# Router logits as fp32r products of split parts, and the last row tile's scaling split between two engines

## The chip, the cores and the metric

One Trainium2 chip, one NeuronCore, one launch. The metric is device time in microseconds (us) of that core, the median of a few runs; lower is better. Five engines work side by side: TensorE (PE; its weight loads have rows of their own, PEld), VectorE (DVE), ScalarE (ACT), GpSimd (POOL) and SyncE (SP, which only issues DMAs here). Each takes its instructions in order and they meet at semaphores.

## The reference, cut to what matters

One layer of a decoder on 1040 prompt rows (16 learned rows and 1024 prompt rows) and 8 sample rows, 1048 in all. After the mixer come the output projection, the residual sum, a norm, and a mixture of experts. Before the experts a router picks for each row one of 4 groups and two of its 8 experts:

```python
x = x + jnp.concatenate([y_a, y_b], axis=-1) @ w_out
h2 = rmsnorm(x, norm_ffn)
lg = h2 @ rg_w + rg_b                      # 4 group logits
le = h2 @ re_w + re_b                      # 32 expert logits
_, gsel = lax.top_k(lg, 1)
ev, ei = lax.top_k(le[group gsel], 2)
wts = softmax(lg)[gsel] * softmax(ev)
out = sum over the two experts e: wts * (silu(h2 @ w_gate[e]) * (h2 @ w_up[e])) @ w_down[e]
```

## The kernel before

The program runs in stages. The mixer fills the first 465 us. The stage that the change touches, `route_parts`, runs from 465 to about 612 us. The experts follow until about 970 us: 32 experts, whose weights stream in from DRAM while TensorE multiplies.

In `route_parts` the 1048 rows are cut into nine tiles, t = 0 to 8, eight of 128 rows and a last one of 24 (`LAST`). The order on each engine is written out by hand:

- TensorE, for tile t, runs eight steps i of six products with 512 columns each (line 2075: the output projection, as fp32r products of a high and a low part of each operand). Between the steps it does work on earlier tiles: at i = 2 `turn(t-1)` transposes the residual row tile (line 2002), at i = 3 `position(t-2)` counts rows per expert (2018, 2021), at i = 4 `score(t-1)` makes the logits (2010), at i = 6 `tabulate(t-2)` writes a table (2027). In tiles 1 and 2 it also carries products for the eight sample rows (1496, 1502).
- VectorE, for tile t, makes `yt_lo` of tile t+2 (1808, 1813), then the residual sum `x` (1913), then waits for the norm's factor and makes the normed rows `h` (1922), then `place(t-1)` (1887 to 1892), then `choose(t)` (1839 to 1881): some 25 small instructions, each waiting for the one before it, that turn logits into chosen experts. In tile 1 `sample.second` (1426 to 1429) stands between `h` and `place`.
- ScalarE makes the high parts for tile t+2 (1745, 1748), then the sum of squares (1774), its logarithm (1776) and exponential (1779), then copies the transposed tile from PSUM into `xtt` (1732, two copies of 512 columns), then two small exponentials for `choose`.

The score of a tile waits for both copies of `xtt`. The transpose of tile t waits for `x` of tile t. At the third tile `position(0)` also waits, through `sample.second_read`, until `sample.second` is done, since both use one PSUM bank. After the ninth tile's product (`prod` reaches 9) SyncE starts the first experts' weights, and what is left of the ninth tile (residual sum, transpose, score, choose, place, tabulate) has to end before the rows of the first experts can be gathered.

## Time and profile before

| | us |
|---|---|
| median of 3 runs | 981.25 (979.59 to 982.6) |
| the profiled execution, its own time | 979.38 |
| its span in the trace | 977.6 |
| TensorE busy in the span | 946.4 |
| VectorE busy | 698.6 |
| ScalarE busy | 491.2 |

The span runs from the first to the last instruction of the profiled execution; 1.8 us lie around it. Matmuls are pipelined, so a busy TensorE is not one at its peak, and a row's duration on TensorE holds a fill and drain that the next one overlaps: spacings of starts tell what one costs. The granted TensorE clock was 0.994 of full speed over the span.

### The profile page before, as it was taken

To read this page: it belongs to the slowest core of one execution; us is meant where nothing else is said; L and a number is where in the kernel's file an instruction comes from. 1 tells how busy PE (TensorE), PEld (TensorE's weight loads), DVE (VectorE), ACT (ScalarE), POOL (GpSimd) and SP (SyncE) were. 2 spreads that over 40 slices of the span, in tenths; PEclk is the share of its full clock that TensorE was granted. 3 is DMA by queue.
4 is the path that set the end of the run, shared out by engine and by line. 5 is a ranking of instruction groups with operands and counts; after the bars stand their busy time and mean duration, and the time that the engine had idled before them with its cause. 6 is when DMAs were issued, how large, how long until landed. Compare 5 with 4: busy or idle time off the path is not lost.

```text
span 977.6 us, 14810 instructions
## 1 busy us (share of the span) xinstructions
PE 946.4 (97%) x5408; PEld 817.8 (84%) x5408; DVE 698.6 (71%) x1059; ACT 491.2 (50%) x890; POOL 191.5 (20%) x153
## 2 busy tenths in 40 slices
PE   5999999999899999999999998999999999999996
PEld 4889999999899999999888885667777777777762
DVE  7466677789453634546666666769999999999996
ACT  7578778432423222232422313246666666666794
POOL 2000000000000000000030001315555555554414
PEclk9999999999999999999999999999999999999999
DMA  7104775623755664446833235999999999999994
GB/s 253 52 22 136 176 160 134 176 88 128 229 135 151 166 165 116 123 145 185 290 103 124 71 112 199 345 407 415 412 415 409 409 400 415 396 413 411 393 396 161
DMA packets 123499, 230.61 MB, mean 236 GB/s; under 512 B 71528, under 2 KB 84386, under 8 KB 114734
## 3 DMA queue, kind: packets, MB, share of 16 engines
q1 hardware_dynamic: 108102, 202.69, 60.0%
q0 software_dynamic: 15264, 26.92, 7.4%
q8 instruction: 37, 0.61, 0.3%
q14 instruction: 24, 0.20, 0.1%
q10 hardware_dynamic: 72, 0.20, 0.1%
HBM read 205.33 MB, written 53.11 MB: 264 GB/s over the span
## 4 chain that ended last, share of the span: by engine, by line
PE 86%; DVE 8%; ACT 3%; DMA 1%; issue 1%; SPq 0%; POOL 0%; POOLq 0%; ACTq 0%; DVEq 0%
PE psum L1157 26%; PE psum L2421 12%; PE psum L2075 10%; PE psum L2511 8%; PE psum L2425 5%; PE psum L2357 3%; PE psum L2405 3%; DVE xi L961 2%; DVE it L959 2%; PE psum L2478 2%; PE psum L1180 2%; PE psum L2010 1%; PE psum L1262 1%; DVE acc L901 1%; PE psum L1249 1%
## 5 line engine op out<-in xcount | busy, mean ns | idle before, releaser
L1157 PE MATMUL psum<-hh,wh 128*128 128x350 f32 x672 | 222.7, 331 | 0.7 <-ACT acc L690 0.7
L1157 PE MATMUL psum<-hh,wl 128*128 128x350 f32 x672 | 217.2, 323 | 0.0
L1157 PE MATMUL psum<-hl,wh 128*128 128x350 f32 x672 | 216.5, 322 | 0.0
L1157 PEld LDWEIGHTS psum<-hh,wh 128*128 128x128 f32 x672 | 127.1, 189 | 2.2 <-ACT acc L690 1.0
L1157 PEld LDWEIGHTS psum<-hl,wh 128*128 128x128 f32 x672 | 126.9, 189 | 0.9
L1157 PEld LDWEIGHTS psum<-hh,wl 128*128 128x128 f32 x672 | 126.6, 188 | 0.0
L2395 DVE TENSOR_TENSOR wgu_lo<-wgu,wgu_hi 128x1536 fp32r<-128x1536 f32 x60 | 105.4, 1758 | 17.1 <-ACT wgu_hi L2390 17.0
L2390 ACT ACTIVATE wgu_hi<-wgu 128x1536 fp32r<-128x1536 f32 x60 | 89.3, 1489 | 2.1 <-DMA new_ssm_sample<-s_in 2.1
L2421 PE MATMUL psum<-wgu_hi,xgt_hi 128*128 128x512 f32 x180 | 85.6, 475 | 0.0
L1702 POOL IOTA r_iw<- 128x8 f32 x1 | 0.1, 144 | 410.5 <-DMA mixer_rows<-th 410.5
L859 DVE TENSOR_TENSOR wl<-wst,wh 128x1024 fp32r<-128x1024 f32 x28 | 34.3, 1225 | 58.8 <-ACT wh L633 58.7
L2349 POOL DMA_INDIRECT sum_rows<-total,slot_rows x32 | 66.5, 2078 | 23.5 <-issue 22.1
L2421 PE MATMUL psum<-wgu_lo,xgt_hi 128*128 128x512 f32 x180 | 70.8, 393 | 0.0
L2421 PE MATMUL psum<-wgu_hi,xgt_lo 128*128 128x512 f32 x180 | 70.7, 393 | 0.0
L2491 DVE TENSOR_TENSOR wd_lo<-wd,wd_hi 128x2048 fp32r<-128x2048 f32 x30 | 68.8, 2292 | 1.2
L2118 POOL DMA_INDIRECT xg<-h_rows,slot_rows x34 | 63.5, 1869 | 24.3 <-DVE slot_rows L1933 10.3
L2343 POOL DMA_INDIRECT before<-sum_rows,slot_rows x34 | 34.4, 1012 | 149.2 <-DVE total L2524 142.9
L2487 ACT ACTIVATE wd_hi<-wd 128x2048 fp32r<-128x2048 f32 x30 | 57.7, 1923 | 0.0
L2425 PE MATMUL psum<-wgu,xgt_rest 128*128 128x512 f32 x120 | 56.3, 591 | 0.0
L2375 ACT ACTIVATE xgt_hi<-psum 128x768 fp32r<-128x768 f32 x30 | 24.4, 813 | 61.6 <-PE psum L2357 61.6
L901 DVE SCALAR_TENSOR_TENSOR acc<-raw,cqw,acc 128x1072 f32<-128x1072 f32 x36 | 48.0, 1334 | 0.9
L2075 PE MATMUL psum<-wo_hi,yt_hi 128*128 128x512 f32 (+1 forms) x144 | 47.8, 413 | 0.0
(376 smaller groups left out, 1887.5 us busy)
## 6 DMA issues: line engine op xcount, KB each, us to landing
wgu<-w_gate SPq DMA_DIRECT2D x34, 1024.0 KB
wgu<-w_up SPq DMA_DIRECT2D x34, 1024.0 KB
wd<-w_down SPq DMA_DIRECT2D x34, 1024.0 KB, 13.6
wst<-w_in SPq DMA_DIRECT2D x28, 512.0 KB, 4.2
ck<-qkv_rows SPq DMA_DIRECT2D x9, 702.0 KB
qkv_rows<-acc SPq DMA_DIRECT2D x12, 520.0 KB, 6.4
xb<-x SPq DMA_DIRECT2D x8, 512.0 KB, 4.3
wo<-w_out SPq DMA_DIRECT2D x8, 512.0 KB, 7.1
```

The source lines that it names most:

```text
L901: stt(ac[:, 0:QLEN], rw[:, q:q + QLEN], w[:, q:q + 1], ac[:, 0:QLEN], ALU.mult, ALU.add).then_inc(taps if q < KQ - 1 else conv_ok, 1)
L1157: ins = mm(ps[:, c, 0:ZC], w[:, kk, :], a[:, kk, c * ZC:(c + 1) * ZC], start=(kk == 0 and q == 0), stop=(kk == KD - 1 and q == 2))
L2075: ins = mm(ps[0:n, 2 * (t % 2) + c, :], y, w[:, c * 512:c * 512 + 512], start=(i == 0 and q == 0), stop=(i == KD - 1 and q == 2))
L2118: pool.indirect_dma_start(b.xg[k][:, :], None, b.h2_dram, bass.IndirectOffsetOnAxis(ap=b.slot_rows[:, e:e + 1].bitcast(U32), axis=0), boun ...
L2349: pool.indirect_dma_start(b.sum_d, rows_of(e), rows[:, :], None, bounds_check=TOK - 1, oob_is_err=False).then_inc(q.sum_out.sem, 16)
L2390: nc.scalar.activation(w_hi[x.p][h][:, :, :, :], half_of(b.slots[x.k][0], h), ACT.Copy).then_inc(w_hi_ok[h][x.p].sem, 1)
L2395: nc.vector.tensor_tensor(half_of(b.slots[x.k][1], h), half_of(b.slots[x.k][0], h), w_hi[x.p][h][:, :, :, :].bitcast(F32), ALU.subtract).t ...
L2421: ins = nc.tensor.matmul(gate_up_bank(x.p), a[:, kk, :], w, start=(kk == 0 and i == 0), stop=(kk == KP - 1 and i == 2))
L2425: nc.tensor.matmul(gate_up_bank(x.p), xt_rest[x.p][:, kk - KP, :], raw[:, :, kk, :], start=False, stop=False)
L2487: nc.scalar.activation(wd_hi[x.p][:, :, :], b.slots[x.k][2][:, :, :], ACT.Copy).then_inc(wd_hi_ok[x.p].sem, 1)
L2491: nc.vector.tensor_tensor(b.slots[x.k][3][:, :, :], b.slots[x.k][2][:, :, :], wd_hi[x.p][:, :, :].bitcast(F32), ALU.subtract).then_inc(wd_ ...
L2511: ins = nc.tensor.matmul(ps[0:C, 4 + 2 * x.p + c, :], h[x.p][:, f, :], w[:, f, c * 512:c * 512 + 512], start=(f == 0 and i == 0), stop=(f ...
```

## The change

The logits were f32 products of the transposed rows `xtt` (stationary, 128 x 128) and the weights `rwf` (36 columns). Now both are split into a part rounded to fp32r and the rest. The high parts of the rows multiply high and low weights side by side (72 columns), the low parts multiply the high weights (36 columns) and add to the first 36. VectorE makes the low part of the rows in `turned_low` and then joins the two halves of the logits with two instructions where it had one. Twice, at the start, VectorE works on the weights (`w_both`). In the ninth tile alone the normed rows are made otherwise: VectorE multiplies the rows by the weights of the norm, ScalarE scales the result by the norm's factor, and ScalarE copies the transposed rows before it takes the logarithm and the exponential.

```diff
-    xtt = m.place("xtt", [P, KD, P])
+    xtt = m.place("xtt", [P, KD, P], F32R)
+    xtt_lo = [m.place(f"xtt_lo{g}", [P, KD // 2, P], F32R, at=at) for g, at in enumerate((b.hist_at, b.state_at))]
+    w_both = m.place("r_w_both", [P, KD, 2, GRP + NE], F32R, at=b.negmask_at)
...
-            if t >= 2:
+            if 2 <= t < T - 1:
                 act.wait_ge(h2_out[t % 2], 16 * (t // 2))
-            a_(h2[t % 2][0:n, :], b.x1[0:n, t, :], ACT.Square, accum_out=b.stat[0:n, t, 0:1]).then_inc(sq.sem, 1)
+            scratch = h2[t % 2] if t < T - 1 else xt[1]
+            a_(scratch[0:n, :], b.x1[0:n, t, :], ACT.Square, accum_out=b.stat[0:n, t, 0:1]).then_inc(sq.sem, 1)
+            if t == T - 1:
+                copy_turned(t)
...
-            copy_turned(t)
+            if t < T - 1:
+                copy_turned(t)
             if t == T - 1:
+                act.wait_ge(rs.sem, rs.at(T))
+                act.wait_ge(weighted.sem, weighted.at(1))
+                a_(h2[0][0:n, :], h2[0][0:n, :], ACT.Copy, scale=b.stat[0:n, t, 2:3]).then_inc(h2_ok, 1)
                 act.wait_ge(h2_ok, T)
                 act.dma_start(b.h2_dram[8 * P:TOK, :], h2[0][0:LAST, :]).then_inc(h2_out[0], 16)
...
-            stt(lg[0:n, :], ps[0:n, 4, 0:GRP + NE], b.stat[0:n, t, 2:3], b.rb[0:n, :], ALU.mult, ALU.add
-                ).then_inc(lg_ok, 1)
-            dve.wait_ge(lg_ok, t + 1)
+            for q, base in enumerate((b.rb, lg)):
+                stt(lg[0:n, :], ps[0:n, 4, (GRP + NE) * q:(GRP + NE) * (q + 1)], b.stat[0:n, t, 2:3], base[0:n, :],
+                    ALU.mult, ALU.add).then_inc(lg_ok, 1)
+                dve.wait_ge(lg_ok, 2 * t + q + 1)
...
+        def turned_low(t):
+            n = rows(t)
+            if t == 0:
+                dve.wait_ge(b.hist_out, 16)
+                dve.wait_ge(b.state_out, 16)
+            for g in range(2):
+                dve.wait_ge(turned_c, 2 * t + g + 1)
+                tt(xtt_lo[g][:, :, 0:n], bank4(ps, 4 + g, P, n), xtt[:, 4 * g:4 * g + 4, 0:n].bitcast(F32), ALU.subtract
+                   ).then_inc(turned_lo.sem, 1)
...
         tt(rwf[:, :, :], b.rw[:, :, :], bc(wft[:, :], GRP + NE), ALU.mult).then_inc(rwf_ok, 1)
+        dve.wait_ge(rwf_ok, 1)
+        V.tensor_copy(w_both[:, :, 0, :], rwf[:, :, :]).then_inc(rwf_ok, 1)
+        dve.wait_ge(rwf_ok, 2)
+        tt(w_both[:, :, 1, :], rwf[:, :, :], w_both[:, :, 0, :].bitcast(F32), ALU.subtract).then_inc(rwf_ok, 1)
...
             if t == T - 1:
+                dve.wait_ge(x1_ok, T)
+                dve.wait_ge(h2_out[0], 16 * 4)
+                tt(h2[0][0:n, :], b.x1[0:n, t, :], wf[0:n, :], ALU.mult).then_inc(weighted.sem, 1)
+                turned_low(t)
                 place(t - 1)
+                dve.wait_ge(rs.sem, rs.at(T))
+                choose(t)
+                break
...
             stt(h2[t % 2][0:n, :], b.x1[0:n, t, :], b.stat[0:n, t, 2:3], wf[0:n, :], ALU.mult, ALU.mult
                 ).then_inc(h2_ok, 1)
+            turned_low(t)
             if t == 1:
                 sample.second(dve)
...
         def score(t):
             n = rows(t)
-            pe.wait_ge(turned_c, 2 * t + 2)
+            pe.wait_ge(turned_lo.sem, turned_lo.at(2 * t + 2))
             for kk in range(KD):
-                ins = mm(ps[0:n, 4, 0:GRP + NE], xtt[:, kk, 0:n], rwf[:, kk, :], start=(kk == 0), stop=(kk == KD - 1))
+                if kk >= 1:
+                    j = kk - 1
+                    mm(ps[0:n, 4, 0:GRP + NE], xtt_lo[j // 4][:, j % 4, 0:n], w_both[:, j, 0, :], start=False, stop=False)
+                if kk == KD - 1:
+                    mm(ps[0:n, 4, 0:GRP + NE], xtt_lo[1][:, 3, 0:n], w_both[:, kk, 0, :], start=False, stop=False)
+                ins = mm(ps[0:n, 4, 0:2 * (GRP + NE)], xtt[:, kk, 0:n], w_both[:, kk, :, :].rearrange("p k e -> p (k e)"),
+                         start=(kk == 0), stop=(kk == KD - 1))
             ins.then_inc(logits, 1)
```

The order of the instructions around it, at three places. First VectorE in the second tile (t = 1), before the change: `h` is the normed rows, the four rows of lines 1426 to 1429 are `sample.second`, 1887 and 1892 are `place(0)`, 1839 begins `choose(1)`. What stands in brackets is what the instruction waits for.

```order
L1922 SCALAR_TENSOR_TENSOR h_189<-x_158,stat,wf 128x1024 [waits x1_act]
L1426 TENSOR_TENSOR uu<-vu,psum 128x32 [waits s_products]
L1427 TENSOR_TENSOR oo<-uu,psum 128x32 [waits s_vec]
L1428 TENSOR_TENSOR oo<-oo,psum 128x32 [waits s_vec]
L1429 TENSOR_TENSOR osq_s<-oo 128x32 [waits s_vec]
L1887 TENSOR_TENSOR r_tmp_194<-r_o_200,psum 128x64 [waits r_pos,s_vec]
L1889 TENSOR_REDUCE r_rank<-r_tmp_194 128x2 [waits r_rank]
L1892 TENSOR_TENSOR r_in_slot<-r_rank,r_ic 128x256 [waits r_vec]
L1839 SCALAR_TENSOR_TENSOR lg<-psum,stat,rb 128x36 [waits logits]
L1847 TENSOR_REDUCE r_one<-lg 128x1 [waits lg_ok]
```

The same place on VectorE in the changed kernel (its line numbers are its own):

```order
L1956 SCALAR_TENSOR_TENSOR h_189<-x_158,stat,wf 128x1024 [waits x1_act]
L1904 TENSOR_TENSOR xtt_lo_191<-psum,xtt 128x512 [waits x1_copied]
L1904 TENSOR_TENSOR xtt_lo_192<-psum,xtt 128x512 [waits x1_copied]
L1427 TENSOR_TENSOR uu<-vu,psum 128x32 [waits s_products]
L1428 TENSOR_TENSOR oo<-uu,psum 128x32 [waits s_vec]
L1429 TENSOR_TENSOR oo<-oo,psum 128x32 [waits s_vec]
L1430 TENSOR_TENSOR osq_s<-oo 128x32 [waits s_vec]
L1910 TENSOR_TENSOR r_tmp_197<-r_o_203,psum 128x64 [waits r_pos,s_vec]
L1912 TENSOR_REDUCE r_rank<-r_tmp_197 128x2 [waits r_rank]
L1915 TENSOR_TENSOR r_in_slot<-r_rank,r_ic 128x256 [waits r_vec]
L1851 SCALAR_TENSOR_TENSOR lg<-psum,stat,rb 128x36 [waits logits]
L1851 SCALAR_TENSOR_TENSOR lg<-psum,stat,lg 128x36 [waits lg_ok]
```

Two subtractions that wait for ScalarE's copies now stand between `h` and `sample.second`, and a second instruction on the logits follows the first. The same two subtractions and the second logit instruction stand in every tile.

Second, VectorE in the ninth tile of the changed kernel:

```order
L1940 TENSOR_TENSOR x_158<-psum,xt_181 24x1024 [waits out_prod,x2_in0,r_vec]
L1947 TENSOR_TENSOR h_188<-x_158,wf 24x1024 [waits h2_out0,x1_ok]
L1904 TENSOR_TENSOR xtt_lo_191<-psum,xtt 128x4x24 [waits x1_copied]
L1904 TENSOR_TENSOR xtt_lo_192<-psum,xtt 128x4x24 [waits x1_copied]
L1910 TENSOR_TENSOR r_tmp_197<-r_o_203,psum 128x64 [waits r_pos]
L1912 TENSOR_REDUCE r_rank<-r_tmp_197 128x2 [waits r_rank]
L1915 TENSOR_TENSOR r_in_slot<-r_rank,r_ic 128x256 [waits r_tabled,r_vec]
L1851 SCALAR_TENSOR_TENSOR lg<-psum,stat,rb 24x36 [waits logits,x1_act]
L1851 SCALAR_TENSOR_TENSOR lg<-psum,stat,lg 24x36 [waits lg_ok]
```

Before, the three instructions of `place(7)` came straight behind `x`, and then `h`, which waited for the norm's factor; now the product with the weights alone comes first, and the factor is waited for by the logits.

Third, TensorE at the score of the second tile in the changed kernel. The semaphore `x_in0` counts the low halves that VectorE has made; before, these places held eight f32 products of 36 columns, the first waiting for `x1_copied`.

```order
L2050 MATMUL psum<-r_w_both,xtt 128x72 [waits x_in0]
L2047 MATMUL psum<-r_w_both,xtt_lo_191 128x36
L2050 MATMUL psum<-r_w_both,xtt 128x72
L2047 MATMUL psum<-r_w_both,xtt_lo_191 128x36
L2050 MATMUL psum<-r_w_both,xtt 128x72
```

## Rows read from the trace of the kernel before

**Rows 1.** The page: busy time of each engine over the span.

```profile
PE 946.4 (97%) x5408; PEld 817.8 (84%) x5408; DVE 698.6 (71%) x1059; ACT 491.2 (50%) x890; POOL 191.5 (20%) x153
```

**Rows 2.** Chain that ended last, 455 to 660 us: start, us, what.

```profile
544.49 0.87 PE psum L2002 x8
...
548.59 1.71 PE psum L2010 x16
...
559.09 0.87 PE psum L2002 x8
...
599.98 1.22 DVE x L1913
...
610.81 0.66 PE psum L2027 x4
```

**Rows 3.** Busy time in a stretch of the experts: PE, PEld, DVE, ACT, POOL, clock, DMA.

```profile
700.00:750.00 50.00, 50.00 (x225) 38.16 (x224) 46.09 (x43) 32.71 (x37) 27.44 (x17) 1.00 1.02 414
```

**Rows 4.** VectorE and the sixth tile's surroundings, 542 to 559 us, order of time.

```profile
545.62 1.28 DVE L1922 SCALAR_TENSOR_TENSOR h<-x,stat,wf 128x1024 f32<-128x1024 f32 x1 [1.78 <-ACT stat L1779]
...
548.20 1.98 PEld L2010 LDWEIGHTS psum<-rwf,xtt 128*128 128x128 f32 x16
...
550.34 0.26 DVE L1839 SCALAR_TENSOR_TENSOR lg<-psum,stat,rb 128x36 f32<-128x36 f32 x1 [2.24 <-PE psum L2010]
...
557.35 1.22 DVE L1913 TENSOR_TENSOR x<-psum,xt 128x1024 f32<-128x1024 f32 x1
...
558.70 1.02 PEld L2002 LDWEIGHTS psum<-ident,x 128*128 128x128 f32 x8
```

**Rows 5.** Weight loads by line (ns min/median/max), and the ninth tile's score.

```profile
L2010 PEld LDWEIGHTS psum<-rwf,xtt x144: 99/192/192, 485.1 to 603.7; 128*128 128x128 f32 x128, 128*24 128x24 f32 x16
...
L2075 PEld LDWEIGHTS psum<-wo_hi,yt_hi x144: 101/188/192, 464.9 to 598.3; 128*128 128x128 f32 x128, 128*24 128x24 f32 x16
...
603.25 0.70 PE L2010 MATMUL psum<-rwf,xtt 128*24 128x36 f32 x16 [0.24 <-ACT xtt L1732]
```

**Rows 6.** VectorE in the mixer's first stage: two subtractions of 512 columns from PSUM.

```profile
14.31 1.28 DVE L854 TENSOR_TENSOR hl<-psum,hh 128x512 fp32r<-128x512 f32 x2
15.51 1.22 DVE L859 TENSOR_TENSOR wl<-wst,wh 128x1024 fp32r<-128x1024 f32 x1
```

**Rows 7.** Timelines of DVE, ACT, PEld and PE around the third tile's start.

```profile
499.96 0.18 DVE L1426 TENSOR_TENSOR uu<-vu,psum 128x32 f32<-128x32 f32 x1
500.61 0.38 DVE L1429 TENSOR_TENSOR osq_s<-oo 128x32 f32<-128x32 f32 x1
506.27 0.25 DVE L1839 SCALAR_TENSOR_TENSOR lg<-psum,stat,rb 128x36 f32<-128x36 f32 x1 [2.04 <-PE psum L2010]
513.80 1.22 DVE L1913 TENSOR_TENSOR x<-psum,xt 128x1024 f32<-128x1024 f32 x1
...
501.12 1.09 ACT L1732 ACTIVATE xtt<-psum 128x512 f32<-128x512 f32 x2 [2.40 <-PE psum L2002]
...
502.52 0.42 PEld L2018 LDWEIGHTS psum<-r_os,before 128*128 128x128 f32 x2
...
515.12 1.06 PE L2002 MATMUL psum<-ident,x 128*128 128x128 f32 x8
```

**Rows 8.** Timeline around the first tile.

```profile
473.90 0.45 DVE L1902 TENSOR_TENSOR rwf<-rw,wft 128x288 f32<-128x288 f32 x1
476.96 1.22 DVE L1913 TENSOR_TENSOR x<-psum,xt 128x1024 f32<-128x1024 f32 x1
479.14 1.03 PEld L2002 LDWEIGHTS psum<-ident,x 128*128 128x128 f32 x8
```

**Rows 9.** Timeline behind the ninth tile's product.

```profile
602.84 0.35 ACT L1732 ACTIVATE xtt<-psum 128x96 f32<-128x96 f32 x2
602.97 1.27 DVE L1922 SCALAR_TENSOR_TENSOR h<-x,stat,wf 24x1024 f32<-24x1024 f32 x1 [0.94 <-ACT stat L1779]
...
604.17 0.24 DVE L1839 SCALAR_TENSOR_TENSOR lg<-psum,stat,rb 24x36 f32<-24x36 f32 x1
```

More of the change, by code:

```diff
@@ L179, in build @@
     b.ones = m.place("ones", [P, P])
+    b.negmask_at = m.at
     b.negmask = m.place("negmask", [P, P])
@@ L1608, in route_parts @@
                                                   s("rwf_ok"))
+    turned_lo, weighted = s.again("x1_turned_lo"), s.again("x1_weighted")
     iota, vr, exped = s("r_iota"), s("r_vec"), s("r_exp")
@@ L1997, in turn @@
                 pe.wait_ge(turned_c, 2 * t)
-                pe.wait_ge(lg_ok, t)
+                pe.wait_ge(lg_ok, 2 * t)
             for g in range(2):
@@ L2061, in tensor @@
                     if t == 1:
-                        pe.wait_ge(rwf_ok, 1)
+                        pe.wait_ge(rwf_ok, 3)
                     score(t - 1)
```

## The prediction

> **What bounds the kernel now.** I read the page's busy times first: TensorE is busy for 97% of the span and no other engine comes near [rows 1]. A busy TensorE need not be the bound, so I took the chain of waits next. From one tile's transpose at 544.49 us to the next one's at 559.09 us it never leaves TensorE [rows 2]: a tile costs 14.60 us and VectorE and ScalarE hide behind it. Only behind the ninth tile's product does the chain change hands: to VectorE at 599.98 us, and through the norm and the choosing of experts back to TensorE at 610.81 us [rows 2]. In the experts TensorE is busy for all 50.00 us of a 50 us stretch, with DMA as busy beside it [rows 3]; SyncE's loads there are started by slots that TensorE frees. So what the change does to the routing stage is passed on to the end one for one: time of TensorE in the tiles, stalls of TensorE in the tiles, and time between 599.98 and 610.81 us.
>
> The reader should look at the slack too, in the timeline of one tile [rows 4]. VectorE ends `x` at 557.35 + 1.22 = 558.57 us; TensorE asks for it at 558.70 us. One tile earlier the slack is 0.26: `h` idled 1.78 us before 545.62, so `x` ended at 543.84, and the transpose's load, 14.60 before 558.70, was at 544.10. From the logits' first instruction (550.34) to the end of `x` VectorE needs 8.23 us with no idle time between: with 0.13 us more the load of the transpose's weights is late, and with 0.1 beyond that (a load's own length, below) its product is. The tile's period on TensorE and the loop through VectorE are almost equal. Any work that VectorE gets in that loop is therefore not free, although its busy share is 71%.
>
> **The score itself.** Before, eight f32 products per tile gave 16 pairs of load and product, which take 1.71 us, 107 ns a pair [rows 2]. Now there are 8 fp32r products of 72 columns and 8 of 36, 16 instructions. In the ninth tile, where the load has 24 columns instead of 128, the same 16 pairs span at most 0.70 us, 44 ns each [rows 5]. So the 128-column load sets the 107 ns, and the number of loads stays 16. Does a fp32r load cost the same? The rows say 188 ns for 128 columns and 101 for 24 (fp32r, line 2075), against 192 and 99 (f32, line 2010) [rows 5]: 0.84 and 0.89 ns a column. A gain from the type is excluded but for a few ns. What the trace does not show is a narrow fp32r product (its narrowest has 350 columns, in line 1157). Lower bound of its cost: hidden under the load, 0 us. Upper bound: it is charged like f32. An f32 product of 36 columns is two pairs, and a pair in the ninth tile, load and all, costs 44 ns; 72 columns would be four such, 176 ns: 8 x (176 - 107) = 0.55 us a tile, 5 us in nine. I take 0.6 us for all tiles, 5 ns a pair, near the lower end, because the nearest rows (the loads) say that the load decides; 0 and 5 stay for the range.
>
> The Trainium skill, "TensorE: Matmul & The Clock Gate", section "Weight-path perf modes", has a rule that speaks for a gain: a load of 128 weights whose type is not FP32 gets the fast weight load, about twice as fast as measured there. By it the pairs would fall toward 53 ns and a tile would save 0.85 us. The rows on fp32r loads do not show it; it is among the rivals.
>
> **The weights' two parts.** VectorE gets a copy and a subtraction of 288 columns behind `rwf`, which took 0.45 us [rows 8]: 2 x 0.45 and two waits, 0.95 us. They push `x` of tile 0, whose end was 476.96 + 1.22 = 478.18 us, to 479.13; the transpose loads at 479.14 [rows 8]. Hidden by 0.01 us: I count 0.05. Without that cover it would be 0.95.
>
> **The low part of the rows, tile 1.** This is the largest term. A subtraction of 512 columns from PSUM into fp32r takes 1.20 us a pair, start to next start [rows 6]. In tile 1 `sample.second` ran from 499.96 to 500.61 + 0.38 = 500.99 us, early, because it needed no transpose. Now it stands behind two subtractions that wait for ScalarE's copies, which start at 501.12 and end at 502.21 [rows 7]. The first subtraction can begin at 501.74, the second waits until 502.24 and ends at 502.92 (0.68 alone); `sample.second` then takes its 1.03 us and ends at 503.9. TensorE's `position(0)` waits for it, because it writes the PSUM bank that `sample.second` reads, and its load was at 502.52 [rows 7]. Behind that wait stands everything of TensorE: the products of tile 2 and its score. From 502.52 to 503.94 is 1.4 us. A load runs ahead of its product (that of tile 5's score is at 548.20, and the chain counts its products from 548.59 [rows 2, 4]); I take 0.15 of that as cover and 1.25 us as lost. VectorE's small instructions are stretched at this time: logits to `x` took 513.80 - 506.27 = 7.53 us here [rows 7] against 7.01 in tile 5 [rows 4]. A subtraction stretched in the same way could make the stall 1.6; with all of the load's lead as cover it is 1.0.
>
> **The joined logits and the loop through VectorE.** The second logit instruction is 0.26 us and one wait: 0.29 us more in `choose`. For tile 2, `x` ended at 515.02 and the transpose's product stood at 515.12 [rows 7], so 0.29 us would be all on the path, but the 1.25 us shift moves `choose(1)` half out of the time in which it was stretched and gives back part of the 0.5 us: 0.1 us. For tiles 3 to 5 the 0.13 to 0.26 us of slack at the load are used up, and the load is 0.03 to 0.16 late, which its 0.1 of cover about hides.
>
> The score now waits for the low halves. `h` starts at 545.62; the pair follows at 546.82 and ends at 548.10, handed over at 548.14, against the score's load at 548.20 [rows 4]: just in time. Counted from the end of `x` (543.84) that is + 4.30 and + 4.36. But TensorE will follow `x` closer: with the transpose's load at + 0.05 to + 0.15 instead of + 0.26, the score's load, 4.10 behind it, is wanted at + 4.15 to + 4.25 and gets its data 0.05 to 0.15 us late, and the product may see that and some of the load's own 0.1. I take 0.45 us over tiles 2 to 5 (0 to 1.2). Tiles 6 and 7 have more slack, since VectorE has `yt_lo` of 24 rows to make there, or none. `place` comes 1.2 us later, but its users on TensorE come four products later or a tile later: nothing.
>
> **The ninth tile.** Before, from the end of `x` (601.20) VectorE did `place(7)`, idled 0.94 us for the norm's factor, did `h` in 1.27 and began the logits at 604.17 [rows 9]. Now the product with the weights (1.2 us) runs while ScalarE squares; ScalarE's copies move ahead of logarithm and exponential, from 602.84 to about 602.3, and end at 602.65; two subtractions of 96 columns, 0.25 us each (a 24 x 36 logit instruction is 0.24), end near 602.95; `place(7)` takes 602.97 - 0.94 - 601.20 = 0.83; the logits begin near 603.8. TensorE's score, released at 602.95, is done by 603.65. That is 0.35 us earlier, less 0.27 for the second logit instruction: 0.1 us gained. ScalarE's scaling (an estimate of 1.1 us, from its copies of 2 x 512 columns in 1.09 [rows 7]) ends at 604.4 and its DMA leaves about 0.15 us later than before; the gather needs it only after 611 us, so it is free. I count 0, between -0.3 and +0.3.
>
> **Sum.** 0.05 + 1.25 + 0.1 + 0.45 + 0 + 0.6 (score) = 2.45 us, slower. On the profiled execution, 979.38 us, that is 981.8; it stands 1.87 us under the median of the runs, so on the median 981.25 + 2.45 = 983.7 us. What a measurement of this kernel can tell from no change is about 0.3%, 2.9 us, and my sum is just inside.
>
> **Rivals.**
> - *The loads get faster (faster).* If fp32r loads of 128 columns no longer bind, a pair falls from 107 toward the ninth tile's 44 ns. A tile then saves up to 16 x 63 ns = 1.0 us, eight tiles 8; VectorE's loop shortens with it, since it begins at the logits. The sum becomes 1.85 - 8 = -6.15: 975.1 us. From 93 ns a pair on (128 pairs x 14 ns = 1.8) it outweighs the rest, and from 70 ns on it is faster by over 0.3%. Against it: load rows alike within 4 ns. The skill's rule on the fast weight load, above, is this rival. Chance 0.07.
> - *Narrow fp32r products are dear (slower).* At 176 ns per 72-column product the score adds 5 us: 981.25 + 1.85 + 5 = 988.1 us. A mild form, 20 to 60 ns a pair, gives 984.5 to 987. For it: no row has one. Against it: an f32 product does four times the passes and fits. Chance 0.2.
> - *VectorE becomes the period.* If each of the two added waits (low halves, joined logits) costs 0.2 us more than I count, tiles 1 to 5 slip by 0.4 each, 2.0 us more: 985.7 us. For it: the slack of 0.13 us; against it: VectorE has 4 us idle in a tile, 1.78 + 2.24, if at other places [rows 4]. Chance 0.13.
> - *The wait in tile 1 is absorbed.* TensorE would have idled or waited near there anyway, or the copies come earlier: the 1.25 goes, 982.4 us, no change to be told. Against it: the chain shows no other wait of TensorE there. Chance 0.1.
>
> My own case has 0.5, with a range of its own from 982.3 to 985.5, of which 0.38 lies within 0.3% (below 984.2) and 0.12 above.
>
> Chances: faster by over 0.3% 0.07 (the first rival, and little else), within 0.3% 0.38 + 0.1 + 0.03 from the mild forms = 0.51, slower 0.12 + 0.17 + 0.13 = 0.42. The range for 8 in 10 leaves out the first rival and the dearest form of the second: 981.2 to 988.0 us.
>
> **What the profile after would show.** The rows of `position` at the third tile start 1.2 to 1.3 us after the projection's products before them, with an idle TensorE released by VectorE's `osq_s`: if TensorE has no idle time there, the largest term is wrong. The 16 rows of the score span 1.7 to 1.8 us; 1.0 would be the first rival, 2.2 the second. The period of tiles 3 to 5 reads 14.6 to 14.9 us. The ninth tile's logits begin 2.6 us behind the end of `x` instead of 2.97. The tabulation that ends the stage comes about 2.5 us later than 610.81. I would be wrong above all through the price of a 72-column fp32r product, which no row shows.

## The result and the profile after

The changed kernel takes 984.29 us, median of 21 runs (978.73 to 994.15), against 981.25 us for the kernel before (21 runs, 978.40 to 983.87). The ratio is 1.0035, with a 95% interval from 1.0021 to 1.0048: slower by 2.1 to 4.7 us, about the size of what can be told from no change. A second set on another chip (the experiment `change_again`) gave 1.0040 [1.0012, 1.0069]. Forecast were 983.7 us and 2.45 us more. A ratio is not the quotient of the two medians printed beside it, and it leaves out three slow executions (994.15 us here, 993.45 us of the kernel before on the chip of `change_again`, 5422.97 us of `copies_first`).

The page's busy times, which answer to [rows 1]:

```profile
PE 949.7 (97%) x5408; PEld 819.4 (84%) x5408; DVE 711.0 (73%) x1088; ACT 491.8 (50%) x891; POOL 192.1 (20%) x153
```

The number of products is the same (5408); VectorE is busy 12.4 us longer. The profiled execution's span is 980.4 us, its own time 982.2 us, the granted clock 0.992.

The chain that ended last, 455 to 660 us (start, us, what), answers to [rows 2]. The eight transposes L2037 mark the tiles; L2059 is `position`, L1904 makes the low halves, L1430 ends `sample.second`:

```profile
479.98 0.87 PE psum L2037 x8
...
502.70 0.45 PE psum L2037 x4
503.17 0.61 ACT xtt L1736
503.80 1.29 DVE xtt_lo L1904 x2
...
505.66 0.39 DVE osq_s L1430
506.09 0.41 PE psum L2059 x2
...
518.69 0.87 PE psum L2037 x8
...
533.29 0.87 PE psum L2037 x8
...
547.99 0.88 PE psum L2037 x8
...
562.81 0.87 PE psum L2037 x8
...
577.53 0.87 PE psum L2037 x8
...
592.14 0.87 PE psum L2037 x8
...
603.92 1.22 DVE x L1940
...
614.96 0.66 PE psum L2068 x4
```

Differences of these starts give the tiles' periods. Here they stand beside those read in the same way from the chain of before and of `change_again`, the same changed kernel profiled again. The last two rows run from the last transpose to the ninth tile's `x` and from there to the tabulation.

| period, us | before | after | `change_again` |
|---|---|---|---|
| to the second tile's transpose | 21.12 | 22.72 | 21.12 |
| to the third's | 14.59 | 15.99 | 15.99 |
| fourth | 14.66 | 14.60 | 14.59 |
| fifth | 14.59 | 14.70 | 14.73 |
| sixth | 14.60 | 14.82 | 14.81 |
| seventh | 14.59 | 14.72 | 14.71 |
| eighth | 14.62 | 14.61 | 14.62 |
| to `x` of the ninth | 11.68 | 11.78 | 11.77 |
| to the tabulation | 10.83 | 11.04 | 11.53 |
| sum | 131.28 | 134.98 | 133.87 |

Three places show. At the third tile 1.40 us are lost in both profiles, and the chain leaves TensorE there, for ScalarE's copy, the low halves and `sample.second`. At tiles five to seven 0.1 to 0.2 us are lost in each. At the second tile 1.60 us are lost in one profile and nothing in the other: that is the clock. (The two periods of the ninth tile are taken up below.) Windows of the profile after (window, then PE, PEld, DVE, ACT and POOL busy, granted clock, DMA share and GB/s):

```profile
486.00:488.00 2.00, 2.00 (x15) 2.00 (x16) 0.14 (x1) 0.00 (x0) 0.00 (x0) 0.79 0.91 356
488.00:490.00 2.00, 2.00 (x6) 1.52 (x6) 1.72 (x9) 0.30 (x2) 0.00 (x0) 0.50 0.03 12
490.00:492.00 2.00, 2.00 (x13) 1.81 (x12) 1.72 (x10) 0.49 (x2) 0.00 (x0) 0.86 0.00 0
```

The granted clock falls to 0.50, TensorE's lower level of 1.2 GHz, in the last products of the first tile's score, and comes back within 5 us. In the timeline the two projection products behind the score take 1.05 us where the same two products take 0.62 elsewhere:

```profile
488.62 1.05 PE L2116 MATMUL psum<-wo_lo,yt_hi 128*128 128x512 f32 x2
...
496.62 0.62 PE L2116 MATMUL psum<-wo_lo,yt_hi 128*128 128x512 f32 x2
```

The waits between 465 and 620 us (engine, tile and line <- releaser: us in total, times, longest):

```profile
PEld psum L2059 <- DVE osq_s L1430: 1.6, 1, 1.6
PE psum L2059 <- DVE osq_s L1430: 1.1, 1, 1.1
PEld psum L2050 <- DVE xtt_lo L1904: 0.9, 3, 0.4
```

And the sixth tile's timeline, which answers to [rows 4], the bracket telling how long the engine was idle and who ended it:

```profile
547.78 0.86 PEld L2037 LDWEIGHTS psum<-ident,x 128*128 128x128 f32 x8 [0.22 <-DVE x L1940]
...
552.04 0.19 PEld L2050 LDWEIGHTS psum<-r_w_both,xtt 128*128 128x128 f32 x1 [0.38 <-DVE xtt_lo L1904]
...
554.06 0.26 DVE L1851 SCALAR_TENSOR_TENSOR lg<-psum,stat,rb 128x36 f32<-128x36 f32 x1 [1.23 <-PE psum L2050]
```

Both of TensorE's waits on VectorE are now real: `x` is 0.22 us late at the transpose's load, the low halves 0.38 us late at the score's. The tile is 0.22 us longer than before, less than the two together.

The ninth tile, answering to [rows 9]:

```profile
603.92 1.21 DVE L1940 TENSOR_TENSOR x<-psum,xt 24x1024 f32<-24x1024 f32 x1
...
606.22 0.35 ACT L1736 ACTIVATE xtt<-psum 128x96 fp32r<-128x96 f32 x2
606.48 0.42 DVE L1904 TENSOR_TENSOR xtt_lo<-psum,xtt 128x96 fp32r<-128x96 f32 x2
...
606.96 0.25 PE L2050 MATMUL psum<-r_w_both,xtt 128*24 128x72 f32 x1
...
607.71 0.23 PE L2050 MATMUL psum<-r_w_both,xtt 128*24 128x72 f32 x1
...
608.05 0.24 DVE L1851 SCALAR_TENSOR_TENSOR lg<-psum,stat,rb 24x36 f32<-24x36 f32 x1 [0.31 <-PE psum L2050]
608.33 0.24 DVE L1851 SCALAR_TENSOR_TENSOR lg<-psum,stat,lg 24x36 f32<-24x36 f32 x1
```

The window in which these products run, in the columns of the windows above:

```profile
606.00:608.00 2.00, 2.00 (x25) 1.87 (x25) 1.57 (x6) 1.94 (x7) 0.58 (x1) 0.66 0.99 418
```

`x` ends at 605.14; ScalarE's copies start 1.08 us behind it, against 1.64 before (602.84 - 601.20), so they did move ahead. The 16 products span 606.96 to 607.94, 0.98 us against 0.70, and the logits begin 2.91 us behind `x`, before 2.97. But the granted clock is 0.66 in this window and 0.50 in the next; in `change_again` it is 0.71 and 0.50 around the same products. In the profile of before it was 1.00 there and fell only behind 610 us. So neither profile of the changed kernel shows its ninth tile at full clock; `one_logit_instruction` and `f32_score`, below, do.

### The profile page after: what moved, and what is told of

Same layout as the page of the kernel before. It is cut to its first block, busy times and chain, and to the rows that moved or that the text cites. A ratio compares the mean times of both kernels' runs of the same rounds, so it can differ in the third digit from the quotient of the medians.

```text
span 980.4 us, 14849 instructions
## 1 busy us (share of the span) xinstructions
PE 949.7 (97%) x5408; PEld 819.4 (84%) x5408; DVE 711.0 (73%) x1088; ACT 491.8 (50%) x891; POOL 192.1 (20%) x153
## 4 chain that ended last, share of the span: by engine, by line
PE 84%; DVE 8%; ACT 4%; DMA 2%; issue 1%; SPq 0%; POOL 0%; POOLq 0%; DVEq 0%; ACTq 0%
PE psum L1158 26%; PE psum L2462 12%; PE psum L2116 10%; PE psum L2552 8%; PE psum L2466 5%; PE psum L2398 3%; PE psum L2446 2%; DVE xi L962 2%; DVE it L960 2%; PE psum L2519 2%; PE psum L1181 2%; PE psum L2050 1%; DMA y<-sum_rows 1%; PE psum L1263 1%; DVE acc L902 1%
```

## The experiments

Each kernel was timed against the kernel before on its own chip; ratios with a 95% interval. Periods come from the chains, read as above.

**`second_first`.** In the second tile `sample.second` goes ahead of the low halves.

```diff
+            if t == 1:
+                sample.second(dve)
             turned_low(t)
-            if t == 1:
-                sample.second(dve)
```

> The changed kernel, with the one difference that in the second tile the four instructions of the sample rows (sample.second) stand ahead of the two subtractions for the low half, as they stood before the change. Theory A (the wait of position(0) for sample.second costs 1.3 us on TensorE's path): the idle time of TensorE ahead of position(0) goes, and the transpose of the third tile follows that of the second after about 14.8 us instead of 16.15; the time falls by 1.0 to 1.6 us against the changed kernel, to about 982.9. Theory B (the changed kernel's extra time is stretches at half clock in the routing stage, and the wait costs nothing that counts): the wait goes but the median stays near 984, and runs still spread from 979 to 989.

Measured: 981.87 us, before 979.23; 1.0020 [1.0004, 1.0035]. The wait of `position` on `osq_s` is gone and the third tile's period is 14.98 us instead of 15.99. But the fourth's is 15.06 instead of 14.60: of the 1.0 us won half comes back. The timeline of GpSimd (POOL) and VectorE shows why:

```profile
501.15 8.78 POOL L1460 TENSOR_TENSOR s_in<-s_in,vals 128x512 f32<-128x512 f32 x8 [80.59 <-PE psum L1497]
...
502.43 0.37 DVE L1430 TENSOR_TENSOR osq_s<-oo 128x32 f32<-128x32 f32 x1
...
508.85 1.09 DVE L1860 SCALAR_TENSOR_TENSOR r_eq<-lg,r_one,r_iw 128x4 f32<-128x4 f32 x1
...
511.30 0.23 DVE L1860 SCALAR_TENSOR_TENSOR r_eq<-r_les,r_one,r_iw 128x8 f32<-128x8 f32 x1
```

`choose(1)` now runs while GpSimd still works (501.15 to 509.93), and its first `r_eq` takes 1.09 us where the next takes 0.23. In the profile after `choose(1)` starts at 509.72 and none of its instructions is stretched. So the wait had given back what the contention costs. The prediction reckoned with half of 0.5 us; this one instruction is 0.86 us longer. In the profile of before two instructions are stretched in its place, together by 0.66 us (`r_eq` 0.39 us for 0.22, `r_og` 0.78 for 0.29).

**`wait_alone`.** The kernel before with only the second tile's wait: two subtractions of the same shape behind the copies, ahead of `sample.second`. Nothing uses their result.

```diff
+                for g in range(2):
+                    dve.wait_ge(turned_c, 2 * t + g + 1)
+                    tt(xtt_lo[g][:, :, 0:n], bank4(ps, 4 + g, P, n), xtt[:, 4 * g:4 * g + 4, 0:n], ALU.subtract)
                 sample.second(dve)
```

> The kernel before, with one addition: in the second tile VectorE waits for ScalarE's copies and makes the two subtractions of 512 columns (nobody reads them) ahead of sample.second, as the changed kernel does there. Score, logits and the ninth tile are those of before. Theory A: TensorE waits ahead of position(0) as in the changed kernel, the third tile's transpose comes 15.8 to 16.0 us behind the second's instead of 14.59, all later tiles keep 14.6, and the kernel is 0.10 to 0.16% slower than before. Rival (the wait is made up for later, by the sample rows' work on GpSimd or in the experts): the gap is there and the time is that of before.

Measured: 982.05 us, before 981.11; 1.0020 [0.9989, 1.0052]. The chain:

```profile
501.37 0.45 PE psum L2008 x4
...
504.33 0.39 DVE osq_s L1429
...
504.77 0.41 PE psum L2024 x2
...
517.36 0.87 PE psum L2008 x8
...
531.95 0.87 PE psum L2008 x8
```

The third tile's period is 15.99 us, as in the changed kernel, and all later ones are 14.59 to 14.62. The wait alone makes the whole of that 1.40 us. Timing does not resolve it.

**`f32_score`.** VectorE's work, both logit instructions and all waits of the changed kernel are kept, but the score is eight f32 products of 36 columns from the rounded rows, without the low parts.

```diff
-                    mm(ps[0:n, 4, 0:GRP + NE], xtt_lo[j // 4][:, j % 4, 0:n], w_both[:, j, 0, :], start=False, stop=False)
...
-                ins = mm(ps[0:n, 4, 0:2 * (GRP + NE)], xtt[:, kk, 0:n], w_both[:, kk, :, :].rearrange("p k e -> p (k e)"),
+                ins = mm(ps[0:n, 4, 0:GRP + NE], xtt[:, kk, 0:n].bitcast(F32), rwf[:, kk, :], start=(kk == 0), stop=(kk == KD - 1))
```

> The changed kernel with f32 products again (36 columns, 8 a tile, from the rounded rows, so the logits lack the low parts), while VectorE still makes the low halves, the score still waits for them and two logit instructions still follow. Theory A: the extra time stays, 983 to 984, with the idle time of TensorE ahead of position(0). Theory B: the extra stretch at half clock in the second tile is absent as in the kernel before, the spread of the runs is that of before, and the median is 981.25 plus the waits' 1.5 to 2, about 983; with B alone and no price for the waits, 981.3.

Measured: 982.92 us, before 979.23; 1.0030 [1.0018, 1.0042], as slow as the changed kernel within the intervals. Its waits between 465 and 600 us are the changed kernel's to the tenth:

```profile
PE psum L2053 <- DVE osq_s L1430: 1.1, 1, 1.1
...
PEld psum L2045 <- DVE xtt_lo L1904: 0.9, 3, 0.4
```

Its periods too: 21.12, 15.98, 14.59, 14.71, 14.84, 14.71, 14.62. The loss is VectorE's work and its waits, not the products. Its ninth tile has the new order, the low halves and two logit instructions, and ran at full clock up to the tabulation: `x` starts at 606.68 us and the tabulation at 617.43, 10.75 us against 10.83 before.

**`products_alone`.** The other way round: no low halves, so the score waits for the copies as before; the eight narrow products read the high halves and write columns that nobody reads (the low parts are left out of the result). Two logit instructions and the ninth tile's order stay.

```diff
         def turned_low(t):
+            return
...
-            pe.wait_ge(turned_lo.sem, turned_lo.at(2 * t + 2))
+            pe.wait_ge(turned_c, 2 * t + 2)
...
-                    mm(ps[0:n, 4, 0:GRP + NE], xtt_lo[j // 4][:, j % 4, 0:n], w_both[:, j, 0, :], start=False, stop=False)
+                    mm(ps[0:n, 5, 0:GRP + NE], xtt[:, j, 0:n], w_both[:, j, 0, :], start=(j == 0), stop=False)
```

> The products of the change alone: VectorE makes no low halves, the score waits for ScalarE's copies as before, and the eight products of 36 columns read the high halves and write columns that nobody reads, so the logits lack the low part of the rows. The second logit instruction and the ninth tile's new order stay. Theory A (VectorE's waits): 0 to 0.1% over the kernel before. Theory B (narrow fp32r products bring a stretch at half clock): 0.2 to 0.35% over it, with a mean granted clock under that of before.

Measured: 981.35 us, before 979.57; 1.0011 [0.9993, 1.0029]. Periods 21.12, 14.83, 14.77, 14.63, 14.64, 14.63, 14.65. No TensorE wait on VectorE is left in these tiles, though `choose` has its second logit instruction. From the fifth tile on a tile costs 0.03 to 0.04 us more than before, here with products that alternate between two PSUM banks. At the third and fourth, where GpSimd works beside `choose`, it costs 0.24 and 0.11 us.

**`one_logit_instruction`.** `second_first` with one logit instruction: the second 36 columns (high rows times low weights) are left out of the logits; products and low halves are as in the change.

```diff
-            for q, base in enumerate((b.rb, lg)):
-                stt(lg[0:n, :], ps[0:n, 4, (GRP + NE) * q:(GRP + NE) * (q + 1)], b.stat[0:n, t, 2:3], base[0:n, :],
+            stt(lg[0:n, :], ps[0:n, 4, 0:GRP + NE], b.stat[0:n, t, 2:3], b.rb[0:n, :], ALU.mult, ALU.add
```

> As second_first, and with one logit instruction where the change has two, so that the logits lack the high rows' product with the weights' low part. Theory A2 (what second_first still costs is VectorE's loop from logits to residual sum being 0.29 us longer in every tile): it falls from 1.002 to 1.000 to 1.001 of the kernel before. Theory A3 (it is the wait for the low halves): no change against second_first, 1.002, and TensorE still waits for the low halves in tiles 3 to 6.

Measured: 978.77 us, before 979.57; 1.0015 [0.9986, 1.0043]. Its chain:

```profile
530.12 0.87 PE psum L2036 x8
...
544.70 0.87 PE psum L2036 x8
...
559.30 0.87 PE psum L2036 x8
...
573.89 0.87 PE psum L2036 x8
```

Periods of 14.58, 14.60 and 14.59 us (and 14.62 for the eighth tile; 14.59 and 14.94 for the third and fourth): those of before, with all 16 fp32r products and all low halves in them. So the products of the real form cost nothing beside a 128-column load (the 16 span 548.80 to 550.51, 1.71 us, as in [rows 2]). Its ninth tile ran at a granted clock of 1.00 (every window from 600 to 610 us), with the 16 products of the changed kernel:

```profile
603.32 0.22 PE L2049 MATMUL psum<-r_w_both,xtt 128*24 128x72 f32 x1
...
603.79 0.20 PE L2049 MATMUL psum<-r_w_both,xtt 128*24 128x72 f32 x1
...
604.09 0.24 DVE L1850 SCALAR_TENSOR_TENSOR lg<-psum,stat,rb 24x36 f32<-24x36 f32 x1
```

The 16 span 0.67 us (603.32 to 603.99), 31 ns from start to start, against 0.70 us for the f32 products: with a load of 24 columns, too, they cost nothing more. The logits begin 2.60 us behind the end of `x` (601.49).

The loss at tiles five to seven needs both edits on VectorE: without the low halves (`products_alone`) or without the second logit instruction (here) it is gone.

**`wide_products`.** The changed kernel with every product of the score three times as wide (216 and 108 columns; the added columns repeat the logits and are not read).

```diff
-                ins = mm(ps[0:n, 4, 0:2 * (GRP + NE)], xtt[:, kk, 0:n], w_both[:, kk, :, :].rearrange("p k e -> p (k e)"),
+                ins = mm(wide, xtt[:, kk, 0:n], bc1(w_both[:, kk, :, :].rearrange("p k e -> p (k e)"), R),
```

> The changed kernel, with every score product three times as wide (216 and 108 columns, the same weights again; the added columns of the result are not read). Theory B (TensorE falls to half clock because the narrow fp32r products keep it little active under their weight loads): the stretch at half clock behind the first tile's score goes in most runs, the spread narrows, the mean granted clock rises, and the median falls by 1.5 to 4 us to 980.5 to 983, as 216 columns cost no more than a load. Theory A (fixed waits alone): no change, 984. Rival C (a fp32r product under its load is charged by its columns): the score's 16 instructions take over 1.9 us and the kernel gets slower by 1 to 3 us.

Measured: 981.86 us, before 979.23; 1.0037 [1.0019, 1.0055]. Periods 21.10, 16.00, 14.62, 14.81, 14.86, 14.80, 14.62: three times the columns cost at most 0.11 us a tile. The stretch at half clock behind the first tile's score is absent from this profile, and the kernel is no faster for it; another one stands at 604 to 608 us.

**`wide_f32`.** The kernel before with its f32 products three times as wide (108 columns).

```diff
-                ins = mm(ps[0:n, 4, 0:GRP + NE], xtt[:, kk, 0:n], rwf[:, kk, :], start=(kk == 0), stop=(kk == KD - 1))
+                ins = mm(ps[0:n, 4, 0:3 * (GRP + NE)].rearrange("p (r e) -> p r e", r=3), xtt[:, kk, 0:n],
+                         bc1(rwf[:, kk, :], 3), start=(kk == 0), stop=(kk == KD - 1))
```

> The kernel before with every f32 score product three times as wide (108 columns, the same weights again, the added columns are not read). If narrow products under 128-column loads are what lets TensorE fall to half clock in some executions, the mean granted clock rises over that of before and the time falls by 0.5 to 2 us. If the stretches come from elsewhere (the idle time behind the ninth tile), nothing changes. If a pass of 108 columns no longer fits under a load, each tile is 0.1 to 0.5 us longer.

Measured: 981.23 us, before 981.11; 1.0001 [0.9976, 1.0026]; periods 14.59 to 14.67. Under a 128-column load the width of the product is free here in f32 as well. The granted clock is not higher for it (median of the runs 0.992, before 0.993).

**`ninth_tile_alone`.** The kernel before with only the ninth tile's new order (product with the weights first, ScalarE's copies ahead of the root, scaling on ScalarE).

```diff
+                tt(h2[0][0:n, :], b.x1[0:n, t, :], wf[0:n, :], ALU.mult).then_inc(weighted.sem, 1)
                 place(t - 1)
+                dve.wait_ge(rs.sem, rs.at(T))
+                choose(t)
+                break
```

> The kernel before with the ninth tile's new order alone (weights' product on VectorE, scaling on ScalarE, copies ahead of logarithm and exponential), score and logits as before. My sum had the ninth tile's logits 0.35 us earlier before the second logit instruction is paid: here that instruction is absent, so 0.3 us faster, 0.03%, not to be told from none. The rival, that the copies do not come earlier than the accumulator is read: the logits begin within 0.1 us of where they began, no change. A gain of 1 us or more would speak for another mechanism.

Measured: 980.28 us, before 979.57; 1.0025 [0.9999, 1.0051]. The timeline:

```profile
602.77 1.21 DVE L1921 TENSOR_TENSOR x<-psum,xt 24x1024 f32<-24x1024 f32 x1 [0.32 <-PE psum L2089]
...
605.08 0.35 ACT L1733 ACTIVATE xtt<-psum 128x96 f32<-128x96 f32 x2
...
605.73 0.70 PE L2024 MATMUL psum<-rwf,xtt 128*24 128x36 f32 x16
...
606.54 0.24 DVE L1847 SCALAR_TENSOR_TENSOR lg<-psum,stat,rb 24x36 f32<-24x36 f32 x1 [0.46 <-PE psum L2024]
...
613.17 0.66 PE L2041 MATMUL psum<-r_spread,r_in_slot 128*128 128x64 f32 x4 [1.35 <-DVE r_in_slot L1900]
```

The logits begin 2.56 us behind the end of `x` (603.98) and the tabulation 10.40 us behind its start, against 10.83: the order by itself gains 0.43 us in the trace. The time does not show it.

**`score_alone`.** The changed kernel with the ninth tile in the old order.

```diff
                 place(t - 1)
-                dve.wait_ge(rs.sem, rs.at(T))
-                choose(t)
-                break
```

> The changed kernel with the ninth tile as it was before (norm's factor first, copies behind it, rows scaled by VectorE), so the split score, its low halves and the two logit instructions alone. My sum had the ninth tile's part at 0, between -0.3 and +0.3 us: the time is that of the changed kernel, 1.003 to 1.004 of before. If the ninth tile's new order were a loss by itself (ninth_tile_alone was 1.0025, with an interval that holds 1), it is 1.001 to 1.002. If it is a gain, the last tile's logits begin 0.4 us later behind the residual sum than in the changed kernel and the whole is slower by as much.

Measured: 983.05 us, before 981.11; 1.0036 [1.0008, 1.0064]. The tabulation comes 12.76 us behind the start of `x` (615.14 against 602.38), with the clock at half in that stretch. That is 1.2 to 1.7 us more than in the two profiles of the changed kernel, which have half clock there as well; how much of it is the order and how much the clock stays open. The 0.43 us of `ninth_tile_alone` are the clean figure for the order.

**`copies_first`.** The changed kernel with the copies ahead of logarithm and exponential in every tile, the low halves ahead of `h`, and `sample.second` first in the second tile.

```diff
-            if t == T - 1:
-                copy_turned(t)
+            copy_turned(t)
...
+            if t == 1:
+                sample.second(dve)
+            turned_low(t)
             stt(h2[t % 2][0:n, :], b.x1[0:n, t, :], b.stat[0:n, t, 2:3], wf[0:n, :], ALU.mult, ALU.mult
```

> The changed kernel with the ninth tile's order of copies in every tile: ScalarE copies the transposed rows ahead of logarithm and exponential, and VectorE makes the low halves in the time in which it would wait for the norm's factor, ahead of the normed rows; sample.second stands ahead of both in the second tile. If what is left in tiles 3 to 6 is the wait for the low halves, their period goes from 14.7 to 14.8 back to 14.6 us; if it is the loop from logits to residual sum, made longer by the second logit instruction, it stays at 14.7 to 14.8 or goes up by the later normed rows. Either way the third tile's gap loses about 1 us of its 1.4, less what GpSimd takes back by stretching VectorE's small instructions. Expected: 1.001 to 1.002 of the kernel before.

Measured: 982.67 us, before 981.11; 1.0001 [0.9974, 1.0029]. Periods from the third tile on 14.89, 14.79, 14.59, 14.61, 14.58, 14.62: the wait at the third tile and the loop's loss are both gone but for 0.4 us, again where GpSimd works. In the periods it repairs nearly all that the change costs, and it gains nothing beyond. No version tried is measurably faster than the kernel before.

**`high_alone`.** Meant as `products_alone`, but the eight narrow products added high rows times high weights a second time to the first 36 columns, and the low parts were left out. The logits were about doubled, and rows went to other experts: TensorE ran 5476 products instead of 5408.

> The changed kernel without the low halves of the rows: VectorE does not make them (18 subtractions less), the score waits for ScalarE's copies as before, and the products of the low halves read the high halves instead, so the logits lack the low part. TensorE's instructions are all there. Theory A (VectorE's waits): nearly all of the extra time goes, 981.3 to 982. Theory B (the products themselves, through the clock): the time stays at 983 to 985 with runs up to 988.

Measured: 1053.54 us, 1.076 [1.0734, 1.0787]. That is the price of another routing and tells nothing of the products; `products_alone` is its mended form.

**`change_again`.** The changed kernel unaltered, on another chip beside three of the kernels above, to see which differences between the first two profiles come back.

> The changed kernel itself, once more, beside the parts of it on the same chip. All theories: 1.0021 to 1.0048 of the kernel before. It is the reference for the other three, and its trace says whether the stretch at half clock behind the first tile's score comes each time: theory B says it does in most executions, theory A that it is chance.

Measured: 982.46 us, before 979.57; 1.0040 [1.0012, 1.0069]. The third tile's 15.99 us and the 14.7 to 14.8 us come back; the half clock behind the first tile's score does not. In the ninth tile it lasts longer instead: the clock is below full from 608 to 616 us, and the chain runs through 24 products of TensorE ahead of `position` (610.93 to 615.99), most of them at 0.50.

## Why the prediction was right, step by step

Forecast were 983.7 us in a range of 981.2 to 988.0, and slower by 2.45 us; measured were 984.29 us and, by the ratio's interval, 2.1 to 4.7 us. The mechanism was the forecast one, VectorE's added work and the waits for it, but one term of the sum, the price of the narrow products, was almost wholly absent. The terms, in us, against the two profiles of the changed kernel, after and `change_again`, the half clock at the second tile left out:

| term | forecast | measured |
|---|---|---|
| weights' two parts | 0.05 | 0 |
| wait at the third tile, with the joined logits there | 1.25 + 0.1 | 1.40 and 1.40 |
| loop over the five tiles behind it | 0.45 | 0.39 and 0.40 |
| price of the narrow products | 0.6 | 0 but for 0.1 ahead of the ninth tile's `x` |
| ninth tile from `x` on | 0 | +0.2 and +0.7, partly at half clock |
| sum | 2.45 | 2.1 and 2.6 |

At full clock the ninth tile from `x` on gains 0.08 us (10.75 us in `f32_score` against 10.83), which makes the sum about 1.8 us, an estimate from these rows. That the medians differ by 3.0 us, so near the 2.45, is in part luck: the 0.6 us that the products do not cost stand in for time that the prediction had no term for.

- *The bound.* TensorE's tile of 14.60 us with VectorE just hidden behind it held: from the fifth to the seventh tile periods rose only where VectorE was late, by the two waits that the sixth tile's rows show.
- *The weights' parts.* They ran from 474.83 to 475.63 in the profile after, `x` of the first tile ended at 479.45, and the transpose loaded at 479.58 without a wait. Hidden, and the copy took 0.31 us, not 0.45.
- *The wait at the third tile.* The largest term, and all of it: TensorE idle 1.1 us and its load 1.6 us before `position`, released by `osq_s`, and 15.99 us also in `wait_alone`. That the wait gives back part of the contention on VectorE was reckoned too: `second_first` shows that without the wait 0.86 us go to one stretched instruction.
- *The loop.* 0.39 and 0.40 us, summed over five tiles: -0.06 or -0.07, 0.11 or 0.14, 0.22 or 0.21, 0.13 or 0.12, and nothing, for the fourth to the eighth. The prediction had the right picture: the second logit instruction uses up the slack, TensorE follows `x` closer, and so the low halves, just in time before, come late. That fits with each edit costing nothing alone.
- *The score itself.* Here is the term that was mis-sized. Type and width are free while the load has 128 columns: 1.71 us for 16, before and after. They are free in the ninth tile too, where the load has 24: 0.67 us for 16 at full clock (`one_logit_instruction`) against 0.70. The 0.98 us of the profile after, 50 ns from start to start, are those products at a falling clock. What does go with them is 0.1 us ahead of the ninth tile's `x`: the period to it is 11.76 to 11.78 us in every profile with fp32r products of the change's width and 11.67 or 11.68 in every one with f32 products of 36 columns; the two kernels with wide products lie between (11.74 and 11.73). Why is open. So of 0.6 us, spread over all tiles at 5 ns a pair, about 0.1 was there. The Trainium skill's rule in "TensorE: Matmul & The Clock Gate", section "Weight-path perf modes", that a 128-weight load not in FP32 is about twice as fast, does not hold for these fp32r loads. The pairs stayed at 107 ns.
- *The ninth tile.* The logits were to begin 2.6 us behind the end of `x`. At full clock they do: 2.60 us in `one_logit_instruction`, which has the products, the low halves and the new order; the new order alone gave 2.56. The 2.91 us of the profile after are the same work with the clock at 0.66 to 0.50.
- *The tabulation* came 4.15 us later by the profile after and not 2.5. From the first transpose on it is 3.70 and, in `change_again`, 2.59 us; the difference between the two is chiefly the 1.60 us at half clock, less what the ninth tile lost in `change_again`. Nor was all of it passed on to the end, as the prediction had it. Behind the tabulation come 32 products on the chain. In before the clock fell in them and they took 5.25 us; after, it had fallen earlier and they took 3.63. The work behind them starts at 619.25 us against 616.73, 2.52 us later.

The rivals: the loads did not get faster, narrow fp32r products were not dear, and the wait in tile 1 was not absorbed. VectorE as the period is what the loop's term shows in small, 0.4 us and not 2.0. The prediction weighed no rival in which the stretches at half clock come at other places or in other number, and that is what its sum leaves open.

What stays open is the rest between the 1.8 us at full clock (2.1 and 2.6 with the ninth tile as profiled) and the 3.4 or 3.9 us of the two ratios. The first interval begins at 2.1 us, just above the 1.8; the second begins at 1.2 and holds it. Among the runs of `change_again` and the three kernels beside it, a straight line through time against mean clock, with a step for each kernel and leaving out clocks under 0.986, gives 0.65 us for each 0.001 of clock and puts the changed kernel 1.6 us above before at equal clock. On the two other chips the same line (0.78 and 0.68 us) gives 1.6 us for `wait_alone`, 1.7 for `score_alone`, 1.5 for `second_first` and 2.8 for `f32_score`. So a part of the difference goes with the granted clock, but not all of it in every kernel.

Whether the change itself brings more half clock isn't shown. The stretch behind the first tile's score stands in 3 of 7 profiles with narrow fp32r products (after, `second_first`, `copies_first`), in none of 5 with f32 ones (`high_alone` left out), and not in `wide_products`. Counting all windows of 2 us from 465 to 622 us, the time missing from full clock is 1.7 us in before and in seven others, and 3.4 us or more in the six that have the fp32r products, the low halves and both logit instructions: after, `change_again`, `score_alone`, `copies_first` and `wide_products` 3.4, `second_first` 5.1. That speaks for the change as a cause, from one profile each. Against it as the cause of the loss stands `f32_score`: 1.7 us there, and a ratio of 1.0030.

## What to carry to other kernels

An engine that is busy for 71% can still have no room: measure the slack at each point where the bounding engine asks for its result, and add up all edits that lengthen one loop before you call any of them free. When work is put ahead of something on an in-order queue, look at who waits for what stands behind it, here a PSUM bank handed over by `sample.second`: that one order cost 1.40 of the 1.8 us that the traces show at full clock. Work on the array that hides under a 128-column weight load was free in type and width here. Before a short tile is called dearer, look at its granted clock: the 0.98 us of the last tile's products were 0.67 at full clock.

## What the runs showed of the hardware

- *The clock moves the time more than this change does.* The changed kernel's 21 runs read 978.7 and 979.7 us at a mean granted clock of 0.996, 981.3 to 982.5 at 0.992, 987.4 to 988.6 at 0.988. That is about 1.1 us for each 0.001, for one and the same kernel. A profile holds one execution, so a stretch at half clock must be taken out before periods are compared; here it was 1.60 us at the second tile, and 0.3 us for the 16 products of the ninth.
- *Small VectorE instructions stretch by up to the length of a GpSimd instruction.* While GpSimd ran eight products of 512 columns in 8.78 us, 1.10 us each, single VectorE instructions grew: `r_eq` (4 columns) from 0.22 to 1.09 us, `r_in_slot` from 0.43 to 1.15 (in the profile after). The Trainium skill, "SBUF — State Buffer", section "SBUF: two separate sides", says that a VectorE instruction with two inputs in SBUF and a GpSimd instruction that reads SBUF lock each other out of a shared port pair for a whole instruction. The lengths agree with it: both have two SBUF inputs, while the logits' instruction, which reads PSUM, stayed at 0.25 to 0.26. One row needs the page's other case, an instruction in a mode with two ports: in the profile of before `r_og`, a TENSOR_SCALAR, took 0.78 us in this stretch against 0.29 elsewhere; that it runs in such a mode no row shows.
- *Fp32r loads behave like f32 loads*, 107 ns a pair with 128 columns, and products of 72, 108 or 216 columns fit beside them within 0.11 us for 16. With loads of 24 columns, 16 fp32r products of 72 and 36 columns took 0.67 us at full clock (31 ns from start to start) and 50 ns each at half clock; eight f32 products of 36 columns, 16 pairs, took 0.70.
